# Batched one-hot rows with the gate in the first index's rows, and one merged first stage, in a two-layer diffusion-transformer step

## The reference

```python
def _trunk_layer(x, cvec, lp, ctx, pos):
    sh1, sc1, gt1, sh2, sc2, gt2 = jnp.split(jax.nn.silu(cvec) @ w_ada + b_ada, 6, axis=-1)
    h = _rmsnorm(x, n1) * (1 + sc1) + sh1
    ... = _split_proj(h @ w_in)          # pooling mixer, gated linear attention, windowed attention
    ...
def _peer(h, wq, subkeys, u, v):         # 8 heads, 128 keys a side, 16384 experts, top 16
    s = jnp.einsum('nhpd,hpkd->nhpk', (hf @ wq).reshape(...), subkeys)
    sv, si = lax.top_k(s, PEER_TOPK)
    ... # top 16 of the pair sums: expert = i * 128 + j, gates = softmax of their scores
    act = jax.nn.gelu(jnp.einsum('td,tkd->tk', xb, u[eb]), approximate=False)
    return jnp.einsum('tk,tkd->td', gb * act, v[eb])
```

## Time and profile before

| | us |
|---|---|
| median of 3 runs (lowest, highest) | 3950.86 (3949.44, 3951.46) |
| span of the profiled execution | 3944.0 |
| TensorE busy in it | 3668.8 (93%) |
| VectorE busy | 2582.7 (65%) |
| POOL busy | 1645.1 (42%) |
| ScalarE busy | 732.8 (19%) |

### The profile page before, as it was taken

The page is one execution under the profiler, slowest core; times in us unless marked ns, Lnnn a source line. Parts: engine busy times, 40 slices in busy tenths (PEclk is TensorE's granted clock), DMA queues, the critical chain, the costliest instruction groups (busy, mean ns, idle before and its releaser), DMA issues. The chain is left out here.

```text
span 3944.0 us, 39966 instructions
## 1 busy us (share of the span) xinstructions
PE 3668.8 (93%) x13726; PEld 2099.9 (53%) x13726; DVE 2582.7 (65%) x5929; ACT 732.8 (19%) x1622; POOL 1645.1 (42%) x1498
## 2 busy tenths in 40 slices
PE   2988888999999999999989887889999999999997
PEld 1545676655555555555445566765555555555543
DVE  5685688777666666677724738878677646556344
ACT  1143355400000000000012535552000000000000
POOL 0030155446556644444502003544777655445340
PEclk7998999999999999999999998999999999999999
DMA  6321234579999999999930131447999999989774
GB/s 218 126 101 46 90 86 145 185 289 405 379 379 369 378 373 378 379 372 353 393 138 2 47 121 54 126 136 256 359 410 410 387 354 354 366 337 359 304 290 160
DMA packets 365386, 1026.96 MB, mean 260 GB/s; under 512 B 30849, under 2 KB 132481, under 8 KB 364417
## 3 DMA queue, kind: packets, MB, share of 16 engines
q0 software_dynamic: 147456, 536.94, 35.5%
q1 hardware_dynamic: 118000, 433.99, 28.9%
q10 hardware_dynamic: 99728, 53.48, 4.8%
HBM read 965.07 MB, written 59.22 MB: 260 GB/s over the span
## 5 line engine op out<-in xcount | busy, mean ns | idle before, releaser
L1859 PE MATMUL ps<-colsT,arena 128*128 128x384 f32 x4096 | 1359.0, 486 | 5.6 <-DMA arena<-in_peer_ut 5.6
L1859 PEld LDWEIGHTS ps<-colsT,arena 128*128 128x128 f32 x4096 | 775.8, 190 | 584.4 <-issue 94.7
L1894 PE MATMUL ps<-arena 128*128 128x512 f32 x1536 | 676.5, 592 | 0.0
L1366 POOL DMA_INDIRECT proj<-in_peer_u,eidx x336 | 478.9, 1425 | 240.9 <-DVE modbc L1560 110.5
L1366 POOL DMA_INDIRECT proj<-in_peer_v,eidx x335 | 361.1, 1078 | 312.7 <-DVE colsT L1571 214.5
L1894 PEld LDWEIGHTS ps<-arena 128*128 128x128 f32 x1536 | 291.8, 190 | 345.2 <-issue 317.6
L1352 POOL TENSOR_SCALAR x<-iota,modbc 128x128 f32<-128x128 f32 x192 | 145.2, 771 | 719.3 <-ACT modbc L1692 551.5
L1560 DVE CUSTOM_DVE_ANT_0 proj<-proj,rows 128x1024 f32<-128x1024 f32 x336 | 399.4, 1222 | 59.0 <-DMA proj<-in_peer_u,eidx 57.2
L1571 DVE SCALAR_TENSOR_TENSOR colsT<-proj,modbc,colsT 128x1024 f32<-128x1024 f32 x330 | 410.1, 1286 | 14.4 <-DMA proj<-in_peer_v,eidx 13.1
L1894 PE MATMUL ps<-arena,rows 128*128 128x512 f32 x768 | 337.8, 592 | 0.0
L1894 PE MATMUL ps<-arena,x 128*128 128x512 f32 x768 | 337.7, 592 | 0.0
(11 more groups left out here) (298 smaller groups left out, 3716.3 us busy)
## 6 DMA issues: line engine op xcount, KB each, us to landing
arena<-in_peer_ut SPq DMA_DIRECT2D x256, 512.0 KB
arena<-in_peer_v SPq DMA_DIRECT2D x256, 512.0 KB
gmat_d<-arena ACTq DMA_DIRECT2D x24, 2048.0 KB, 9.3
arena<-gmat_d SPq DMA_DIRECT2D x64, 768.0 KB
proj<-in_w_adaT SPq DMA_DIRECT2D x48, 512.0 KB
modbc<-in_w_adaT SPq DMA_DIRECT2D x30, 512.0 KB, 3.7
rows<-in_w_adaT SPq DMA_DIRECT2D x18, 512.0 KB, 3.5
arena<-in_w_in SPq DMA_DIRECT2D x2, 4224.0 KB, 16.6
```

What stands on the lines that cost most here:

```text
L1366: pool.indirect_dma_start(ring[slots[at]], None, tab, bass.IndirectOffsetOnAxis(ap=eidx[:, b * SLOTS + q:b * SLOTS + q + 1], axis=0)).then ...
L1859: mm = pe.matmul(ps[:, 2 + j % 2, 0:ND], utab[:, j % UR, k], hT[:, k, NG:T], start=(k == 0), stop=(k == KT - 1))
L1894: mm = pe.matmul(ps[:, Y_BANKS[2 * d + c2], :], wT[j % CR][:, d * P:(d + 1) * P], vtab[:, j % VR, c2 * 512:(c2 + 1) * 512], start=(j == 0) ...
```

## The change

There are two parts.

**Start.** Load stage and first stage are one, without the barrier between. SP loads x, ident, the bias columns, all 16 tiles of `w_adaT` (each to a place of its own), `w_a` and the other constants; ScalarE's queue loads c, stores silu(c) and loads it back. In the stage only the latents' row is dotted (16 dots), with the norm of the rows after the fourth; the columns are finished in two lots of four k. ScalarE copies the prompt's turned rows as they are and applies the latents' modulation. The prompt's 16 dots come at the head of layer 0's mixer stage on VectorE, then its columns and the modulation of its 128 columns of h in eight instructions. Meanwhile TensorE does the latent halves of ak, aq0 and aq1, waits for the prompt's h, and does the three prompt halves. SP's loads of further tiles (and all behind them) and POOL's clearing of `proj` wait for the prompt's dots.

**Placing**, both layers. VectorE marks the second indices of eight tokens in one instruction and without the gate. The gate goes into the first indices' markers: on POOL as the second operation in place of a constant one; on ScalarE as the bias of the last operation, which is now one instruction a token (gate - 2 |index - slot|, floored at zero). One copy in place of two makes `ijgT`.

```diff
--- before.py
+++ after.py
-A_GRP, B_TOK = 4, 16
+A_GRP, B_TOK, B_SET = 4, 16, 8
...
-    with nc.Block() as block:
-        @block.sync
...
-            for dst, src in loads:
-                sp.dma_start(dst, src).then_inc(loaded, 16)
-            sp.wait_ge(loaded, 16 * len(loads))
...
-    barrier()
-
...
-    FIRST_TILES = [m * KT + k for k in range(KT) for m in range(2)]
+    FIRST_TILES = [(m, k) for k in range(KT) for m in range(2)]
+    first = [ada[:, i] for i in range(ADA_RING)] + [region(arena, i * D, D) for i in range(8)] + [region(proj, i * D, D) for i in range(3)]
+
+    def first_dot(dve, c, v, i):
+        m, k = FIRST_TILES[i]
+        c.wait()
+        ins = dve.tensor_tensor_reduce(out=ada_junk, in0=first[i], in1=silu[:, v], scale=1.0, scalar=0.0, op0=ALU.mult, op1=ALU.add,
+                                       accum_out=ada_col(0, v, m * KT + k))
+        c.done(ins)
...
@@ the first stage, SP's queue
+            sp.dma_start(xb, a["x"].rearrange("b p d -> p b d")).then_inc(x_landed, 16)
+            sp.dma_start(ident[:, :], a["ident"]).then_inc(loaded, 16)
+            sp.dma_start(acols[:, :], a["acols"]).then_inc(loaded, 16)
+            for i, (m, k) in enumerate(FIRST_TILES):
+                sp.dma_start(first[i], a["w_adaT"][0, m * KT + k]).then_inc(first_landed[k], 16)
+            sp.dma_start(w_a, a["w_in"][0, :, 0:A_W].rearrange("(k p) n -> p k n", p=P)).then_inc(win_landed, 16)
...
+            sp.wait_ge(win_landed, 16)
@@ the first stage, ScalarE
-            act.dma_start(w_a, a["w_in"][0, :, 0:A_W].rearrange("(k p) n -> p k n", p=P)).then_inc(win_landed, 16)
-            act.wait_ge(loaded, 16)
+            act.dma_start(csm, a["c_rows"].rearrange("v (p k) -> p v k", k=KT)).then_inc(c_landed, 16)
+            act.wait_ge(c_landed, 16)
             act.activation(cex, csm, ACT.Exp, scale=-1.0).then_inc(exp_done, 1)
+            act.wait_ge(silu_done, 1)
+            act.dma_start(silu_d[0].rearrange("(v p k) -> p v k", v=2, k=KT), csm).then_inc(stored, 16)
+            act.wait_ge(stored, 16)
+            act.dma_start(modbc[:, 0:2 * D], bass.AP(tensor=silu_d.tensor, offset=0, ap=[[0, P], [1, 2 * D]])).then_inc(silu_landed, 16)
+            act.wait_ge(x_landed, 16)
             row_sums(act, c)
             act_rstd(act, c, n1_sums, ms_ready, y_ready, ms, yy, zz)
             for k in range(KT):
-                act.wait_ge(col_ready, k + 1)
+                act.wait_ge(n1_turned, k + 1)
+                act.activation(hT[:, k, 0:P], ps[:, 2 * (k % 4), 0:P], ACT.Copy).then_inc(raw_prompt, 1)
+                act.wait_ge(col_ready, k // 4 + 1)
                 turned_latents(act, mTs[0], k)
@@ the first stage, VectorE
-            dve.wait_ge(n1_sums, NB)
-            normed_rows(dve, c)
             dve.wait_ge(silu_landed, 16)
-            for i, n in enumerate(FIRST_TILES):
-                dve.wait_ge(w_landed[i % ADA_RING], 16 * (i // ADA_RING + 1))
-                ada_dots(dve, c, 0, n, ada[:, i % ADA_RING], (silu[:, 0], silu[:, 1]), ada_junk)
...
+            for k in range(KT):
+                if k == 2:
+                    dve.wait_ge(n1_sums, NB)
+                    normed_rows(dve, c)
+                dve.wait_ge(first_landed[k], 32)
+                first_dot(dve, c, 1, 2 * k)
+                first_dot(dve, c, 1, 2 * k + 1)
...
+                if k % 4 == 3:
+                    first_columns(dve, c, 1, k - 3, k + 1)
                     dve.sem_inc(col_ready, 1)
-                    turned_prompt(dve, mTs[0], k)
...
@@ layer 0, mixer stage: SP (POOL waits likewise), TensorE, VectorE
                 if l == 0:
+                    sp.wait_ge(row_dots, 1)
                     for i in range(ADA_RING):
                         load_ada(i)
...
+                else:
+                    for i, n in enumerate(("ak", "aq0", "aq1")):
+                        segment(n, 1, w_a, i * P, P)
+                    pe.wait_ge(hT_dve, KT)
+                    for i, n in enumerate(("ak", "aq0", "aq1")):
+                        segment(n, 0, w_a, i * P, P).then_inc(u_mm, 1)
...
+                else:
+                    for i in range(len(FIRST_TILES)):
+                        first_dot(dve, c, 0, i)
+                    first_columns(dve, c, 0, 0, KT)
+                    dve.sem_inc(row_dots, 1)
+                    for k in range(KT):
+                        dve.tensor_scalar(hT[:, k, 0:P], hT[:, k, 0:P], mT[:, 0, 1, k:k + 1], mT[:, 0, 0, k:k + 1],
+                                          ALU.mult, ALU.add).then_inc(hT_dve, 1)
@@ both layers, placing stage: POOL, VectorE, ScalarE, TensorE
-                        pool.tensor_scalar(agrp[n % A_GRP][:, t], iota128[:, :], ijgT[:, d % 2, 0, 4 * q + t:4 * q + t + 1], 0.0,
-                                           ALU.add, ALU.is_equal).then_inc(p_made, 1)
+                        tok = 4 * q + t
+                        pool.tensor_scalar(agrp[n % A_GRP][:, t], iota128[:, :], ijgT[:, d % 2, 0, tok:tok + 1],
+                                           ijgT[:, d % 2, 2, tok:tok + 1], ALU.is_equal, ALU.mult).then_inc(p_made, 1)
...
-                    for t in range(16 * step, 16 * step + 16):
+                    for t in range(16 * step, 16 * step + 16, B_SET):
                         n = d * P + t
-                        if n >= B_TOK and t % 4 == 0:
-                            dve.wait_ge(g_mm, (n - B_TOK) // 4 + 1)
-                        dve.tensor_scalar(bring[:, n % B_TOK], iota128[:, :], ijgT[:, d % 2, 1, t:t + 1],
-                                          ijgT[:, d % 2, 2, t:t + 1], ALU.is_equal, ALU.mult).then_inc(b_made, 1)
+                        if n >= B_TOK:
+                            dve.wait_ge(g_mm, (n - B_TOK + B_SET) // 4)
+                        dve.tensor_tensor(bring[:, n % B_TOK:n % B_TOK + B_SET],
+                                          iota128[:, :].unsqueeze(1).to_broadcast([P, B_SET, NKEY]),
+                                          ijgT[:, d % 2, 1, t:t + B_SET].unsqueeze(2).to_broadcast([P, B_SET, NKEY]),
+                                          ALU.is_equal).then_inc(b_made, 1)
...
-                    c.link(act.activation(ijgT[:, d % 2, 0], ps[:, 0, 0:P], ACT.Copy, scale=-1.0))
-                    act.activation(ijgT[:, d % 2, 1:3].rearrange("p a t -> p (a t)"), ps[:, 0, P:3 * P], ACT.Copy).then_inc(tr_out, 1)
+                    act.activation(ijgT[:, d % 2].rearrange("p a t -> p (a t)"), ps[:, 0, 0:3 * P], ACT.Copy).then_inc(tr_out, 1)
+                    act.wait_ge(tr_out, d + 1)
...
-                        c.done(act.activation(four[:, t], iota128[:, :], ACT.Abs, bias=ijgT[:, d % 2, 0, 4 * q + t:4 * q + t + 1]))
+                        tok = 4 * q + t
+                        c.done(act.activation(four[:, t], iota128[:, :], ACT.Abs, scale=-1.0, bias=ijgT[:, d % 2, 0, tok:tok + 1]))
                     c.wait()
-                    act.activation(four, four, ACT.Relu, scale=-1.0, bias=1.0).then_inc(a_made, 1)
+                    for t in range(4):
+                        tok = 4 * q + t
+                        act.activation(four[:, t], four[:, t], ACT.Relu, scale=-2.0,
+                                       bias=ijgT[:, d % 2, 2, tok:tok + 1]).then_inc(a_made, 1)
...
-                            pe.wait_ge(a_made, n // 2 + 1)
+                            pe.wait_ge(a_made, 4 * (n // 2) + 4)
...
-                        pe.wait_ge(b_made, 4 * n + 4)
+                        pe.wait_ge(b_made, 4 * n // B_SET + 1)
```

More of the change, by code:

```diff
@@ L184, in build @@
     wo_landed, wb_landed, st_landed = sem("wo_landed"), sem("wb_landed"), sem("st_landed")
+    first_landed = [sem(f"first_landed{k}") for k in range(KT)]
+    c_landed, row_dots, raw_prompt, ones_set = sem("c_landed"), sem("row_dots"), sem("raw_prompt"), sem("ones_set")
     ada2_landed = [sem("ada2_landed0"), sem("ada2_landed1")]
@@ L267, in build, with first_columns @@
     exp_done, silu_done, col_ready = ev["i_done"], ev["j_done"], ev["k_done"]
-    csm, cex = region(proj, 0, 2, KT), region(proj, 2 * KT, 2, KT)
-    FIRST_TILES = [m * KT + k for k in range(KT) for m in range(2)]
+    csm, cex = region(proj, 3 * D, 2, KT), region(proj, 3 * D + 2 * KT, 2, KT)
+    amask_in = region(arena, 15 * D, 2 * P)
+    FIRST_TILES = [(m, k) for k in range(KT) for m in range(2)]
[6 more added lines that the diff above has]
+        c.done(ins)
+    def first_columns(dve, c, v, k0, k1):
+        both, scales = mTs[0][:, v, 0:2, k0:k1], mTs[0][:, v, 1, k0:k1]
+        c.wait()
+        c.link(dve.tensor_tensor(both, both, b_cols[0][:, 0:2, k0:k1], ALU.add))
+        c.link(dve.scalar_tensor_tensor(out=scales, in0=scales, scalar=1.0, in1=n_cols[0][:, 0, k0:k1], op0=ALU.add, op1=ALU.mult))
     def normed_rows(dve, c):
@@ L338, in _ @@
             c = Chain(dve, dve_step)
+            dve.memset(ones[:, :], 1.0).then_inc(ones_set, 1)
+            dve.memset(lofs[:, :], 0.0).then_inc(ones_set, 1)
             dve.wait_ge(exp_done, 1)
@@ L518, in _ @@
```

(25 more changed lines are left out.)

54 lines of the change are left out of this document (14 added, 40 removed).

## The result

| | us |
|---|---|
| before, median of 4 runs beside it (lowest, highest) | 3950.15 (3945.36, 3951.46) |
| after, median of 4 runs (lowest, highest) | 3971.95 (3970.17, 3976.57) |
| ratio, 95% interval | 1.0057 [1.0042, 1.0071] |
| predicted | 3948 (3924 to 3963) |
| span of the profiled execution, before and after | 3944.0 and 3968.8 |

The change makes the kernel 0.6% slower; the time lies 9 us above the top of my range. One thing on the profiles first: in every run of a changed kernel an execution's own time is 1.8 above its span (after: 3970.6 and 3968.8), and in those of before 2.1 to 2.2. So the profiled execution of before stood for about 3946, not for 3950.9. The spans differ by 24.8, the medians by 21.8.

The account below looks back on a forecast made before the run. TensorE was taken to bound the main loops, so its earlier start and its idle time in the placing counted: 3950.9 - 33.4 for the start + 30.8 for the placing = 3948 us, range 3924 to 3963.

Parts of the forecast that it names:

- signs of being wrong: Gaps staying at 1.18 or going, PEclk under 1 in steady steps, POOL's markers ending after ScalarE's spread, first projection after 55.
- signs of being right: Included gaps of about 1.8 ahead of group 3, placing idle in layer 0 about 57, VectorE ready before latent matmuls end.
- Start, -33.4 forecast: First stage: TensorE's first projection starts at 48.8 in place of 82.21, 33.4 us earlier, all of it kept.
- silu(c) at 17: First stage: c loaded at 4.0, its silu stored by 10.0, and the 1 MB load back, taking 7, done at 17.
- Prompt's dots hidden, cover 1 to 2 us: Layer 0's mixer: VectorE's prompt work takes 21 to 22 us, TensorE's latent matmuls 22.8, so TensorE waits for nothing.
- Placing's idle time, +30.8 forecast: Placing, both layers: ScalarE's longer marks make it 30.8 us slower in sum, 14 to 45 by the bounds.
- 34 gaps x 0.62 = 21.1: Placing: four Relus add 0.62 (bounds 0 and 0.9) to each gap ahead of the last group, from 1.18 to 1.8.
- 9.7 for first steps and scores: Placing: ScalarE's marks add 4.8 at later blocks' first steps, 4.4 in layers' first blocks, 0.5 at steps copying scores.
- VectorE's relief worth nothing: Placing: batched markers save VectorE 1.8 x 48 steps, 86 us, valued at nothing because VectorE already waited for TensorE.
- The rival that VectorE held the placing up: Placing: gaps don't grow, cost nothing or up to 20 back, 3917 down to 3897; relief or a better start 0.25.
- POOL late only from 4 us a group on: Placing: POOL needs 2.8 + 1.2 of 7.8 us a group; rival that it comes late, 3965 to 3989, chance 0.08.
- The clock: Placing: rival that TensorE's clock falls in each longer gap, 34 x 1.7 = 58 us, giving 4006; chance 0.05.

Follow-up runs that it names:

- dve_set_only: Kernel before with only VectorE's markers batched by eight tokens, the gate left out; 3957.4 us, ratio 1.0015.
- dve_token: Changed kernel with VectorE marking token by token again, the gate still in the first index's rows; 3966.5 us, ratio 1.0043.
- set_pairs: Changed first stage with before's placing, ScalarE's spreads in pairs and VectorE's markers batched, the gate left out; 3901.3 us, ratio 0.9880 to before.
- start_early: Changed first stage with SP's loads held until silu(c) is stored, before's placing with ScalarE's spreads in pairs; 3890.6 us, ratio 0.9845 to before.
- pool_imm: Changed kernel with POOL's marker comparing against an immediate again, the gate left out of POOL's groups; 3971.3 us, ratio 1.0050 to before.

## Why the prediction was wrong

The time came out 24 above the forecast. By the profiles the start fell short by 7.5, the placing cost 13.2 more, and the other stretches 6.6 (4.8 of them ahead of the placing of layer 0): 27.3. From this 5.1 go off, since I put 6.9 on the span where the changed kernels' runs have 1.8, and 1.4 come on, since the profiled execution of after lies under its median: 23.6. Two of my signs of being wrong came: a PEclk under 1 in a steady step, and a first projection later than 55. Of the signs of being right the gap of 1.8 with the spread ending just before came, and the 57 of idle time ahead of the placing's matmuls; VectorE wasn't ready before TensorE's latent matmuls ended.

- **Start, -33.4 forecast, -25.9 measured.** The failed step is "silu(c) at 17": it was 23.7. Beside the loads c took 6.3 where I took 3.2, the store 7.7 where I took 4.7. Only the load back (7.9 for 7) was near. The dots added 16 x 0.12 = 1.9, and 0.4 more between the pairs: each waits for the one before, while the 1.15 that I used came from pairs, which wait only every second time. The root's steps (2.8 for 3.8) and ScalarE's last columns (3.3 for 4.0) gave 1.7 back. The Trainium skill's rule in "DMA: Bandwidth & Descriptors", "Queues, rings and completion order" made me choose the low half of the store's bounds. The runs agree that a small transfer does not wait for another queue's whole backlog: eight tiles issued from 5.33 to 12.65 took 17.4 to land (median), the store issued among them 7.7. But the loads made it slow all the same: 6.3 and 7.7 beside them, 1.9 and 1.6 without.
- **Prompt's dots hidden, cover 1 to 2 us.** They took 1.26 too long; the same 0.12 a dot is more than that.
- **Placing's idle time, +30.8 forecast, +30.3 measured.** The 34 gaps x 0.62 = 21.1 were right: 32 of them grew by 0.64, to 1.82, and one Relu gives back 21.6 of idle time. The 9.7 for first steps and scores hit the size by luck. I laid them on ScalarE's longer marks; the runs, in the order in which they took the edits back, lay 5.2 on VectorE's sets and 3.9 on POOL's second scalar, both of which make POOL late. The lower end of my "14 to 45" doesn't follow from the bound of 0 for the Relus either: no mark is longer then, and at most the 0.5 for the scores is left.
- **VectorE's relief worth nothing.** Wrong by the 8 that the sets cost: there was nothing to gain, as I had it, and something to lose. The rival that VectorE held the placing up (0.25) is refuted by `dve_set_only`, `dve_token` and `set_pairs`.
- **POOL late only from 4 us a group on.** In the steady steps right. At the blocks' starts, where four markers follow four, it was late, and I had priced that nowhere in the forecast. With one scalar a marker POOL's mean is 0.97 to 0.99 us in the four kernels with the sets and 0.80 to 0.82 in those without; with two scalars it is 1.07 in after and 0.91 in `dve_token`. By the Trainium skill, "SBUF — State Buffer", "Who interferes with whom", a VectorE instruction with two SBUF inputs contends with a GpSimd instruction that reads SBUF. The sets are such an instruction, and the runs agree; it speaks against the change, and I gave it 0.08.
- **The clock.** This is the term that was missing, and the failed step in the placing: 13.7 of slower matmuls stood at nothing. I priced it only as a fall in each gap (58 us) and gave it 0.05, since a gap of 1.18 showed none. It did not fall in each gap. Some 10 of the 13.7 lie at the blocks' starts, where the clock was low before too and now is for longer, which none of my rivals had. The rest, 3.2, are two single steady steps; before has no low clock in that stretch of layer 0 (window, TensorE alone):

```profile
586.00:673.90 87.90, 76.34 (x443) 1.00 0.52 156
```

After, one such step of `u_stage` and placing, first the timeline, then windows of 4 us (stretch, busy PE, PEld, DVE, ACT, POOL, PEclk, DMA share, GB/s):

```profile
639.73 1.84 PE L1914 MATMUL ps<-x,modbc 128*128 128x128 f32 x8 [1.82 <-POOL x L1375]
```

```profile
633.00:637.00 4.00, 4.00 (x25) 3.14 (x24) 0.92 (x8) 1.45 (x4) 1.21 (x2) 1.00 0.99 280
637.00:641.00 4.00, 2.18 (x15) 2.02 (x15) 1.23 (x1) 3.97 (x13) 3.93 (x4) 0.87 0.99 281
641.00:645.00 4.00, 4.00 (x37) 3.50 (x37) 3.39 (x2) 1.99 (x6) 3.48 (x2) 0.70 0.29 94
645.00:649.00 4.00, 4.00 (x14) 2.29 (x13) 3.93 (x3) 0.00 (x0) 4.00 (x4) 1.00 0.00 0
```

A gap of 1.82 ended at 639.73. By the windows the clock is down behind it, and the eight matmuls there took 1.84 in place of 1.13. Other gaps of 1.82, such as that at 588.15, were followed by none. Summed, TensorE ran at 1.2 GHz for 102 us of after's two placings and for 72 of before's. One Relu in place of four took 21.6 of idle time and 7.7 of busy time away, and the low clock fell from 102 us to 89. What isn't settled is why a given gap tips it and another doesn't, and with that why the placing alone ran 11 us longer in its windows than the same placing behind the changed start. That was not tried: it would need TensorE kept at work in the gaps, in a bank that nothing else holds.

## What to carry to other kernels

Ask whose row of work ends a wait, and check a named releaser against its own end; then ask what is second, since an edit measured alone can read zero (POOL's scalar, 0.7) and cost in full (7.2) once the first is mended. In a stage where TensorE idles often, price a microsecond of idle time above one: here it moved the time by 1.3 (spreads in pairs, 36 for 27) to 1.9 (the sets in `set_pairs`, 13.4 for 7.1). The difference is matmuls at the low clock, and where a gap goes altogether, matmuls that run on. And before cutting or batching instructions, look at the order of the ones that stand in the gap: moving one mark behind a pair of spreads was worth 36 us, more than all the merging in this change.

## What the hardware showed that I had not expected

- An 8 KB transfer on ScalarE's queue takes 1.6 to 1.9 us alone (`start_early`), and 6.3 to 7.7 while x and the 512 KB tiles load on SP's queue (after).
- POOL's 128x128 marker takes 0.71 with one scalar and an immediate and 0.79 with two scalars per partition (medians of `pool_imm` and after); a single one took up to 3.9 us in after, with VectorE's sets in the program, and 2.4 in before.
- Behind 24 gaps of 1.82 between busy stretches TensorE's clock was low twice in one kernel and seven times in another with the same stage; behind 96 gaps of 1.18 never.
- VectorE's 1024-element comparison of two tiles takes 1.23 (after); one Relu of 512 elements holds ScalarE 0.54 to 0.63 (before), four of 128 hold it 1.18 (after).
- Programs with nearly identical mixer work differ by 7.6 us in it (393.8 in before to 401.4 in `start_early`), nearly all of it in TensorE's busy time: a change at the start of a kernel can't be judged from one later stage.
